# Block 2 reordered with PSUM sums, norms by halves, other gather order, and four v rows of each group added by VectorE

## The reference, cut to what matters

```python
def _conformer_conv(a, gate, conv_dw, conv_b, conv_ln_g, conv_ln_b):
    h = a * jax.nn.sigmoid(gate)
    pad = (CONV_W - 1) // 2        # CONV_W = 31 taps, 512 channels
    h = lax.conv_general_dilated(h, conv_dw.astype(h.dtype), window_strides=(1,),
        padding=((pad, pad),), dimension_numbers=('NWC', 'WIO', 'NWC'),
        feature_group_count=CONV_CH)
...
def _peer(xn, peer_wq, peer_keys, peer_u, peer_v):
...
        top_s, pos = lax.top_k(cand_s, PEER_TOPK)          # 16 experts per head and token
        e = jnp.take_along_axis(cand_i, pos, axis=-1)
        g = jax.nn.softmax(top_s, axis=-1).astype(xc.dtype)
        u = peer_u[e]
        h = jax.nn.gelu(jnp.einsum('cd,chkd->chk', xc, u))
        return jnp.einsum('chk,chkd->cd', g * h, peer_v[e])
```

## Time and profile before

| what | value |
|---|---|
| median of 3 runs | 1312.83 us (1311.0 to 1312.92) |
| the profiled execution | 1310.15 us |
| its span in the trace | 1308.3 us |
| busy: TensorE, VectorE, ScalarE, GpSimd | 81%, 55%, 31%, 69% of the span |
| v matmuls of TensorE (L919) | 468.8 us |
| GpSimd splits (L1809) and gather issues (L1847) | 385.1 us; 247.2 + 240.5 us |
| dots on VectorE (L1721) | 299.2 us |
| bytes read from HBM | 355.10 MB, 272 GB/s over the span |

### The profile page before, as it was taken

How to read it: one execution, slowest core, us unless ns; L and a number is a source line. 1 busy time by engine, 2 the same in 40 slices (tenths; PEclk the granted TensorE clock), 3 DMA queues, 4 the chain that set the end, 5 groups by cost and what they waited for, 6 DMA issues and landing times. The chain is left out here.

```text
span 1308.3 us, 15510 instructions
## 1 busy us (share of the span) xinstructions
PE 1059.4 (81%) x5312; PEld 737.4 (56%) x5312; DVE 725.4 (55%) x1651; ACT 408.5 (31%) x711; POOL 901.7 (69%) x849
## 2 busy tenths in 40 slices
PE   5999989999999878989776776777767777767777
PEld 5989879899988876789622222222222232222222
DVE  3435323221161598649677656676567638677443
ACT  4345444444433524354322220222202220122202
POOL 5864437688889658547477777777777776777741
PEclk9999979999999979899999999999999999999999
DMA  6533223445545332035699999999999999999994
GB/s 231 192 133 126 97 97 129 160 180 191 186 171 194 127 129 97 2 115 200 209 411 409 409 409 410 410 410 410 409 410 409 409 409 409 409 409 409 410 409 167
DMA packets 86893, 356.97 MB, mean 273 GB/s; under 512 B 9649, under 2 KB 9777, under 8 KB 76721
## 3 DMA queue, kind: packets, MB, share of 16 engines
q0 software_dynamic: 73728, 268.47, 51.7%
q1 hardware_dynamic: 12672, 86.15, 18.5%
q10 hardware_dynamic: 432, 1.57, 0.3%
HBM read 355.10 MB, written 1.05 MB: 272 GB/s over the span
## 5 line engine op out<-in xcount | busy, mean ns | idle before, releaser
L919 PE MATMUL bank<-v_row,diag 128*128 128x512 f32 x1000 | 468.8, 613 | 183.8 <-DMA v_row<-peer_v_dram,expert 182.2
L1809 POOL TENSOR_TENSOR w_lo<-raw,w_hi 128x512 fp32r<-128x512 f32 x300 | 385.1, 1317 | 187.7 <-ACT w_hi L1010 187.2
L919 PEld LDWEIGHTS bank<-v_row,diag 128*128 128x128 f32 x1000 | 183.0, 192 | 469.4 <-issue 317.8
L1721 DVE CUSTOM_DVE_ANT_0 u_row<-u_row,bank 128x1024 f32<-128x1024 f32 x256 | 299.2, 1218 | 181.5 <-DMA u_row<-peer_u_dram,expert 179.4
L1847 POOL DMA_INDIRECT u_row<-peer_u_dram,expert x256 | 247.2, 966 | 98.4 <-issue 72.3
L1847 POOL DMA_INDIRECT v_row<-peer_v_dram,expert x256 | 240.5, 939 | 91.7 <-issue 73.5
L580 PE MATMUL bank<-hT_hi,w_hi 128*128 128x256 f32 x672 | 192.3, 286 | 4.1 <-DVE hT_lo L1294 4.1
L581 PE MATMUL bank<-hT_lo,w_hi 128*128 128x256 f32 x672 | 190.8, 284 | 0.0
L582 PE MATMUL bank<-hT_hi,w_lo 128*128 128x256 f32 x672 | 190.7, 284 | 0.0
L1010 ACT ACTIVATE w_hi<-raw 128x2048 fp32r<-128x2048 f32 x79 | 150.8, 1910 | 111.9 <-PE bank L582 111.9
L1208 ACT ACTIVATE gelu<-dots 128x16 f32<-128x16 f32 x16 | 3.5, 216 | 501.8 <-DVE dots L1721 501.8
(11 more groups left out here) (233 smaller groups left out, 1355.7 us busy)
## 6 DMA issues: line engine op xcount, KB each, us to landing
raw<-stream_dram SPq DMA_DIRECT2D x79, 1024.0 KB, 4.8
u_row<-peer_u_dram,expert POOLq DMA_INDIRECT x256, 14.4
v_row<-peer_v_dram,expert POOLq DMA_INDIRECT x256, 15.0
residual<-x_in_dram SPq DMA_DIRECT2D x2, 512.0 KB, 5.0
out_dram<-residual SPq DMA_DIRECT2D x4, 256.0 KB, 2.1
consts<-consts_in_dram SPq DMA_DIRECT2D x1, 840.0 KB, 9.8
gain<-norm_final_dram ACTq DMA_DIRECT2D x1, 512.0 KB, 5.4
gain<-norm_g_dram ACTq DMA_DIRECT2D x1, 512.0 KB, 3.7
```

The lines of the kernel that those rows point to most:

```text
L919: ins = mm(accs[half][:, :], diag[:, 2 * m + i, :], row[:, half * 512:(half + 1) * 512], start=False, stop=True, skip_group_check=True)
L1721: ins = v.tensor_tensor_reduce(out=row_of_u, in0=row_of_u, in1=hn_tile[t][:, :], scale=1.0, scalar=0.0, op0=ALU.mult, op1=ALU.add, accum_o ...
L1809: ins = nc.gpsimd.tensor_tensor(w_lo[r][:, cols], raw[r][:, cols], w_hi[r][:, cols].bitcast(F32), ALU.subtract)
```

## The change

It has five parts.

- Norms. ACT squares each half (512 columns) of a tile separately and makes the root with a bias, so that VectorE's `var` step is gone; VectorE scales by halves. Norm 0 needs no `params` for it. The double norm between the blocks has 16 small ACT steps. `BRIDGE` goes from 20 to 14 before norm 2 and from 22 to 10 before the mean.
- Block 2. The order is conv0, conv1, kv, q20, q21, conv2, conv3. The accumulators of VectorE's taps lie in PSUM. Both query turns come ahead of the attention, TensorE's taps are three per step from the second step, VectorE's 8, 8, 6, 6, 4, 4 and then six per step, and GpSimd does its conv taps ahead of the splits of wp0 to wp2. The PSUM banks are planned by hand.
- Scores. `hn` is computed by GpSimd, and choice 0 reads its scores from the PSUM bank.
- Gathers. The last two pairs of u of group 0 wait for late splits instead of the last query. All u of group 1 come ahead of all v of group 0. In the last group the v rows go into the u buffers, and the last row has its own semaphore. VectorE's late splits are in another order.
- Adds. From group 1 on VectorE multiplies pairs 2 and 5 of v (four rows) by their weights and adds them to a running sum `v_sum` in PSUM, between the dots of the next group. TensorE does the other six pairs and adds `v_sum` once for each token tile. In the last group VectorE does pairs 2, 5, 6 and half of pair 7.

```diff
+FIRST_TAPS = (1, 3)
+TAP_BANK = (2, 0)
...
-SHARE = (2, 4, 6)
+SHARE = (2, 5, 6, 7)
...
+DVE_PAIRS = (2, 5)
+PE_PAIRS = (0, 1, 3, 4, 6, 7)
+DVE_ROWS = 4
+ADD_BESIDE = {(2, 1): 0, (3, 0): 1, (5, 1): 2, (6, 0): 3}
...
-            + [f"conv{c}" for c in range(CC)] + ["kv", "q20", "q21"] + [f"wp{q}" for q in range(4)]
+            + ["conv0", "conv1", "kv", "q20", "q21", "conv2", "conv3"] + [f"wp{q}" for q in range(4)]
...
-BRIDGE = {0: 0, 1: 8, 2: 20, 3: 8, "mean": 22, "branch": 8}
+BRIDGE = {0: 0, 1: 8, 2: 14, 3: 8, "mean": 10, "branch": 8}
...
+        def v_used(h, m):
+            if h == 0:
+                return v_free, m + 1
+            if m in DVE_PAIRS:
+                return v_added, 1 + DVE_ROWS * (h - 1) + 2 * DVE_PAIRS.index(m) + 2
+            return v_free, BATCHES + len(PE_PAIRS) * (h - 1) + PE_PAIRS.index(m) + 1
...
+            pe.wait_ge(v_added, 1 + DVE_ROWS * (NH - 1))
+            for half in range(2):
+                mm(mix_bank[0][half][:, :], ident, hn[:, 0, half * 512:(half + 1) * 512], start=False, stop=True,
+                   skip_group_check=True).then_inc(mix_done, 1)
...
+            def square(source, t, half, n):
+                settle(activation(full[:, 2 * t + half, :], source, ACT.Square, accum_out=sumsq[:, half, n:n + 1]))
+            def first_part(n):
+                settle(activation(column(var, n), sumsq[:, 0, n:n + 1], ACT.Copy, scale=1.0 / D, bias=EPS))
+            def root_of_sums(n):
+                activation(column(root, n), sumsq[:, 1, n:n + 1], ACT.Sqrt, scale=1.0 / D,
+                           bias=column(var, n)).then_inc(root_done, 1)
...
+                        ins = first_tap(v, acc(c), c)
                     else:
                         dve.wait_ge(dve_step, at_step[c])
-                        ins = next_tap(v, conv_a[:, c, :], tap, c)
+                        ins = next_tap(v, conv_a[:, c, :] if tap == TAPS - 1 else acc(c), acc(c), tap, c)
...
+            def conv_input(c):
                 bank = ps.full(dve, ("conv", c))
                 dve.wait_ge(conv_sig, c + 1)
                 ps.empty(v.tensor_tensor(conv_in[:, c, PAD:PAD + T], bank[:, 0:T], conv_b[:, c, :], ALU.mult), ("conv", c))
                 ps.copied(dve, ("conv", c))
-                if c:
-                    conv_taps(11)
+            conv_input(0)
+            conv_taps(lead)
+            conv_input(1)
+            conv_taps(8)
...
-                conv_taps(3)
...
+            for c in range(2, CC):
+                conv_input(c)
+                conv_taps(4)
...
+            def add_v(g, j, total):
+                i = 2 * DVE_PAIRS[j // 2] + j % 2
+                if j % 2 == 0:
+                    dve.wait_ge(v_in[i // 2], g * PAIR_IN)
+                dve.wait_ge(v_added, g * DVE_ROWS + (j + 1 - 2 * DVE_ROWS))
+                v.scalar_tensor_tensor(total, v_rows[i][:, :], mixw[:, i:i + 1], v_sum[:, :], ALU.mult,
+                                       ALU.add).then_inc(v_added, 1)
...
+            settle(v.tensor_copy(hn_tile[0][:, :], hn[:, 0, :]))
             late_split(NGRAN - 4)
             choose(1, 1)
             late_split(NGRAN - 3)
+            late_split(NGRAN - 2)
             dot_products(0, 0, range(0, 2))
-            late_split(NGRAN - 2)
-            dot_products(0, 0, range(2, 4))
             late_split(NGRAN - 1)
-            dot_products(0, 0, range(4, BATCHES))
+            dot_products(0, 0, range(2, BATCHES))
...
-            before = GRANULES.index("wp2") + 1
+            before = GRANULES.index("conv3") + 1
...
                     done += 1
-            low_parts(before, NGRAN - LATE)
+            low_parts(before, NGRAN - LATE - 2)
+            pool.wait_ge(gain2_done, 16)
+            for t in range(TT):
+                pool.wait_ge(normed, 2 * TT * len(TURNED) - 2 * TT + 2 * t + 2)
+                nc.gpsimd.tensor_tensor(hn[:, t, :], xs[:, t, :], gain2[:, :], ALU.mult).then_inc(hn_done, 1)
+            for n in range(NGRAN - LATE - 2, NGRAN - LATE):
+                low_part(n, n % RING)
...
             for m in range(BATCHES):
-                if m == EARLY_U:
-                    ps.full(pool, ("query", NH - 1))
+                if m >= EARLY_U:
+                    pool.wait_ge(late_split_done, LATE - RING + 1 + m - EARLY_U)
                 fetch_u(0, m, m + 1)
...
             for m in range(BATCHES):
                 fetch_u(1, m, BATCHES + m + 1)
+            ps.full(pool, ("query", NH - 1))
+            for m in range(BATCHES):
                 gather(peer_v, v_rows, v_in, 0, m)
+            def both(g):
+                pool.wait_ge(experts_ready, g + 1)
+                for m in range(BATCHES):
```

More of the change, by code:

```diff
@@ L214, in gate_beside, with halves_in_order @@
     return None
+def halves_in_order(name):
+    halves = [(t, half) for t in range(TT) for half in range(2)]
+    return halves if name in (None, "down") else sorted(halves, key=lambda x: x[1])
 def nkeys(kind, t):
@@ L246, in attention @@
                 ps.plan("T", ("y", kind, 0))
+            if kind == "G" and s == FIRST_TAPS[0]:
+                ps.plan(None, ("taps",), bank=1)
         ps.plan("T", ("y", kind, 1))
@@ L1295, in low_of_norm, with residual @@
                                          hT_hi[where].bitcast(F32), ALU.subtract), name)
[L1297 to L1303 removed]
+            def residual(name, then=None):
+                for t, half in halves_in_order(name):
                     bank = ps.full(dve, (name, t, half))
@@ L1743, in _ @@
             choose(0, 0)
+            for t in range(TT):
+                ps.copied(dve, ("norm", 3, t, 1))
+            settle(v.tensor_copy(hn_tile[0][:, :], hn[:, 0, :]))
             late_split(NGRAN - 4)
```

409 lines of the change are left out of this document (219 added, 190 removed).

## The result

The changed kernel takes 1289.3 us (median of 4 runs, 1287.29 to 1291.1) against 1312.22 before: a ratio of 0.9826, with a 95% interval of 0.9809 to 0.9843. It is 23 us faster; some 40 were forecast (1273, range 1263 to 1288), so the direction was right and the size was not. The profiled execution took 1287.29, its span is 1285.3.

The account below looks back on a forecast made before the run. The DMA queues were taken to bound the expert stage. Experts sooner 25.6, gathers' start 9.8, adds 0 and tail 2.8 made 38.2 off 1310.15, so 1272.0, set at 1273 for the median; 8-in-10 range 1263 to 1288.

Parts of the forecast that it names:

- The adds, "hidden, worth 0 on both engines": Expert groups: VectorE's four adds, about 1.3 us each, fit under the DMA time and change nothing: 0.
- the cover: Expert groups: 5 us of VectorE slack per group to hide the adds; an add over 2.5 us would use it up.
- A gather costs 1.28 us: Expert stage: 32 gathers take 40.9 us with the DMA queues full, so each costs 1.28 us.
- Block 2, 21.0: Block 2 up to the mean: new order and PSUM accumulators remove TensorE's waits; 21.0 us sooner, bounds 14 and 23.
- the shorter bridge before norm 2: Ahead of norm 2: 14 bridge steps instead of 20 leave TensorE idle, which could bring the half clock.
- Norms 0 and 1, 2.5 by the start of block 2: First two norms: squaring by halves gains 1.0 in norm 1; sums without `params` gain 1.5 in norm 0.
- Norm 3 and the scores, 2.1 together: Before the experts: norm 3 by halves gains 1.0; hn on GpSimd with scores read from the bank gains 1.1.
- The start, 9.8: Gathers' start: second group's first gather 29.2 us after the experts instead of 39.1; taken as 9.8, bounds 6 and 13.
- The tail, 2.8: Behind the last v row: fewer matmuls and sums, 8.8 us instead of 11.6; gain 2.8, bounds 1 and 4.
- The rule against the row: VectorE's taps: the skill's table adds 65 ns per PSUM tap, some 1275 in all; the rows say PSUM costs nothing.
- PSUM does not free the taps, or the clock falls: Rival in block 2: taps still collide with GpSimd or the clock falls; gain 0 to 14, 1280 to 1294; chance 0.15.
- Adds hold GpSimd: Rival in the expert groups: adds delay GpSimd's gather issues, net 16 slower, near 1327; chance 0.04.

Follow-up runs that it names:

- e4: Changed kernel without VectorE's four adds per group, TensorE adding all 16 v rows; last group left as is: 1277.66 us, ratio 0.9735.
- e5: The e4 kernel plus seven one-column memsets per group on VectorE, loop body 266 instructions: 1285.63 us, ratio 0.9775.
- e12: No adds, hn on VectorE, idle matmuls in norm 3 and at attention's head: 1391.8 us with slow gathers, beside 1408.7 for the kernel before.
- e7: Changed kernel with the accumulators of VectorE's taps back in SBUF, in the new order: 1311.14 us, ratio 0.998.
- e8: The e4 kernel with hn on VectorE, 13 idle steps in norm 3, ACT's turned k and q copies ahead of table load and split: 1275.12 us.
- e1: Changed kernel with the hn products back on VectorE behind norm 3 and GpSimd's low parts in one row: 1288.73 us, ratio 0.9806.
- e2: Changed kernel with idle matmuls in TensorE's gaps in norm 3, behind the query turns and in attention's second step: 1294.02 us.
- e18: No adds, hn on VectorE, 13 idle steps between norm 3's turns, gathers at 410 GB/s: 1271.75 us, ratio 0.9682.

## Why the prediction was wrong, step by step

- **The adds, "hidden, worth 0 on both engines".** This step failed, and with it the sentence that it rests on, that nothing inside a group is worth anything unless it stops GpSimd from issuing. 0 was forecast, and the adds cost 11.6 us (e4), more than any other step by itself. Their work was sized rightly (1281 to 1290 ns each, 1.3 forecast; no issue behind the start of the stage took over 1.2 us, as before), and the cover was there. What I left out is that the loop's body also grows, from 245 to 269 instructions, and that fetched code takes the same road as the gathers. Per packet it comes to about 1.0 us: from e4 to e5 5 packets and 5.7 us more from the 17th row's landing to the last's, from e4 to the changed kernel 10 packets and 9.6 us (639.1, 644.8, 648.7). The kernel before had 26 packets and 643.6, so against it the stage lost only 5.2: without the adds it would have gained 4.7, which nobody forecast. Without this term the forecast of 1273 would have stood beside 1277.7.
- **A gather costs 1.28 us.** Right for fifteen engines and in every window; the end is set by the sixteenth, which in the kernel before was already alone for the last 10 us. This window of the kernel before shows it, and it stood behind the last slice of the earlier trace rows, whose 167 GB/s I did not look into:

```profile
1286.00:1296.00 10.00, 9.84 (x23) 3.99 (x21) 4.61 (x5) 0.00 (x0) 0.00 (x0) 1.00 0.08 34
```

- **Block 2, 21.0.** Measured 17.2 in the profiled execution (107.4 to 90.2 us from its first matmul to the mean, which before starts at 550.7 and not at 550.9). The seven granules went as forecast (41.9, 41.6 forecast), and the taps too (0.48 with nothing long). Too small was the q tiles' cost: their products have two SBUF operands and stood beside a split, so tile 0 took 9.1 instead of 5.5. ACT, which waited for it, was late with its chain, and attention started at 491.9, not 489.4; the half clock of its first steps, of which e12 got 1.3 us back, was not in the sum either. And these 17.2 hold some luck. The prediction named the shorter bridge before norm 2 as a place where the clock could fall. In the profiled execution it did not, but it did in eight of the eleven traces at 410 GB/s, with the same program up to there: their first 8 us of block 2 have a granted clock of 0.65 to 0.70, and the mean comes 92.4 to 92.7 us after the start (e7 and e8, which change that stage, left aside), not 90.2. The changed kernel first, then e4:

```profile
443.00:451.00 8.00, 8.00 (x67) 8.00 (x68) 5.43 (x12) 6.28 (x6) 4.45 (x4) 1.00 0.01 2
440.30:448.30 8.00, 8.00 (x49) 8.00 (x50) 4.03 (x9) 4.28 (x4) 4.46 (x4) 0.70 0.01 2
```

  That the bridge is the cause is not tested.
- **Norms 0 and 1, 2.5 by the start of block 2.** Measured 0.35 in the profiled execution, but this number is one draw: in the eleven traces at 410 GB/s block 2 starts between 439.8 and 444.5, and before at 443.3. Norm 1 gave its 1.0. In norm 0 the reciprocal on VectorE still stood until 9.08 for `params`, a step that I said was freed; tile 1 was scaled from 11.55 instead of 12.96 all the same, and TensorE's first product with weights came 1.1 sooner (16.70, 17.79 before). In this execution that was waited away at GpSimd's splits, 2.65 us at 25.3, with a granted clock of 0.81 behind it; in e4's it was kept.
- **Norm 3 and the scores, 2.1 together.** Measured -4.1: from the mean to the first scores 49.4 instead of 45.1, and 0.2 gained behind it. The step that failed is that I gave `hn` to GpSimd at no cost for VectorE; the collision price was in my own rows (1.44 against 0.40) and I used it only where the change removed it. 2.1 us are the held scaling (e1), 2.4 the halved clock (e2's norm 3). With both mended, e18 is 5.9 faster than e4, and its first gather follows the mean by 57.0 us where the kernel before has 57.4 and the changed kernel 61.5. So 0.4 of the forecast 2.1 came even then; where the other 1.7 went is open.
- **The start, 9.8.** Measured 13.0, the upper bound: the wait went whole. The splits fell where I had them, but the two issues that they stretch in the middle took 2.10 and 1.90 us instead of 3.06, so the 16th gather went 24.6 behind the first instead of some 29.
- **The tail, 2.8.** Measured 1.8.
- **The rule against the row** went as the rows said: 483 ns for the median tap in PSUM, 485 in SBUF before.
- **The rivals.** "PSUM does not free the taps, or the clock falls" was half right, in the clock: 2.4 us at the first query granule, at least 1.3 at the head of attention, and in most executions some 2.2 at the start of block 2. "Adds hold GpSimd" was wrong: what held was their code, and it held a DMA engine.

Of the 16.3 us, read in the two profiled executions, the stage with its packets (5.2 against 0 from the second group's start to the last row), norm 3 with its scores (6.2), block 2 (3.8), norms 0 and 1 (2.2) and the tail (1.0) make 18.4, and the start gave 3.2 back; the medians differ by another 1.0. The parts ahead of the stage move by some 2 us from one execution to the next, so their shares are known no better than that; the stage with the adds takes 654.7 to 655.4 us in six traces, and the start 25.8 in all eleven.

## What to carry to other kernels

Where a stage is bound by its DMA queues, count the code as well as the work: compare the packets of the instruction queue, and not the loop bodies alone, and look at the last slice, where a stretch at a sixteenth of the rate means that one engine carries more than its share. A product that is moved to GpSimd is not free for VectorE; price it with the rows of the collision that one is about to remove elsewhere. And where two engines slow each other in SBUF (1.57 us for the longest tap beside a split, 0.49 with the accumulator in PSUM), an accumulator that moves to PSUM can do more than a new order does.

## What the runs showed of the hardware

- Packets of q14 (8 KB) delay the gathers' last DMA engine by about 1.0 us each while all engines are busy: 0.34 us for the packet itself, and 0.33 more for each of the two gather packets behind it (0.50 and 0.49 instead of 0.16 to 0.17). Why those two are slow is open.
- Loop bodies of 245, 266, 269, 284 and 290 instructions on VectorE had 21, 26, 31, 31 and 32 packets in the whole program. The length alone does not set the number: the kernel before has the same 245 as e4, and 26 packets against 21. What does was not tried.
- TensorE with 12 matmul rows instead of 16 in a group had a granted clock of 0.82 instead of 0.99 in the expert stage, and the gathers lost nothing by it.
- Two scalings of 128x512 on VectorE took 3.78 us beside GpSimd's product of two SBUF operands, and 1.69 without it.
